# Order of the value products and place of the gate chain in the mixer of a two-layer hybrid block

## Chip, cores and metric

One core of a Trainium2 chip (trn2) runs the whole program. The metric is device time in microseconds (us), 2345.51 us before the change as the median of three runs (2344.53 to 2345.94).

## The reference

Two layers process 256 latent and 256 context tokens of width 1024. Each layer has a gated feed-forward block, a token mixer and a second feed-forward block, with a normalisation behind each. The change concerns the input projection of the mixer and the gates of its mLSTM branch:

```python
(sb, scg, sx, mq, mk, mv, mo, mg, dq, dk, dv, gs, gm, gd) = split_cols(u @ w_in + b_in)
...
g = mg.astype(jnp.float32).reshape(b, t, 4, ML_HEADS).transpose(2, 0, 3, 1)
gates = (g[0], g[1], jax.nn.log_sigmoid(g[2]), jax.nn.log_sigmoid(g[3]))
...
bcum = jnp.cumsum(fc, axis=-1)
d_log = jnp.where(lower, bcum[..., :, None] - bcum[..., None, :] + ic[..., None, :], -jnp.inf)
m_t = jnp.maximum(m_inter, jnp.max(d_log, axis=-1))
```

`mv` are the values (1024 columns, 4 heads), `mg` the 16 gate columns. From the gates come running sums and a running maximum over the tokens, forward and backward; this maximum (the stabiliser) enters the exponentials of the mLSTM scores.

## The kernel before

**Products.** TensorE (PE) multiplies in fp32r, each product in three passes: high part by high part, low by high, high by low. A weight chunk comes by DMA into one of two `raw` buffers. ScalarE (ACT) rounds it into `w_hi` (line 1631) and VectorE (DVE) subtracts to get `w_lo` (line 2365). There are four `w_hi`/`w_lo` slots, so the function `ahead`, called at the step of chunk r, splits chunk r+4 and first waits until chunk r has been multiplied. The DMA of a chunk waits until the chunk two before it has been split.

**The stretch of the change.** `proj_order` writes the order of the steps by hand, and each engine goes through it in order. Behind four `mk` chunks come twelve `mv` steps, and in the list each of these sixteen steps has a number n from 0 to 15, so `mv` step i is n = i+4. The values are made in three groups of four steps, `VALUE_TILES`: here the tokens are the rows of the result, the four token tiles t lie in PSUM banks 0 to 3, and each step adds two of the eight k tiles to all four banks (24 matmuls). The first group is 272 columns wide (256 value columns and the 16 gate columns), the second 512, the third 256.

At a group's last step DVE copies the four banks out to `vaug`, adding the bias (`values`, line 2960). PE starts the next group, or the next chunk in that bank, when the bank is out. Behind the third group come `sx` 1 (bank 0), `sb` 1 (bank 1), four transposes of gate rows (`gates_turn`, line 1434) and `cg` 2, which takes bank 0 again once DVE has evacuated `sx` 1 to `zpad` (line 2913). Then come the mLSTM scores, the second tile of which waits for `em` on ACT (line 1951).

**The gate chain.** `GATES_BEHIND` says behind which n each part of the chain stands. Part 0: PE transposes the gate columns (line 1428), ACT adds the bias, DVE takes absolute values. Part 1: ACT does Exp and Ln (lines 1942 and 1943, each with a table load), then DVE subtracts and copies, with the backward half reversed (lines 2998 to 3002). Part 2: two scans on DVE. Part 3: sums and the transposes' input on DVE (lines 3017 to 3022). Part 4: DVE makes the stabiliser's rounded and reversed copies and the low parts in `neg_g` (lines 3026 to 3030). Parts 0 and 1 stand behind n = 8, the others behind 9, 12 and 15. On every engine a step's `ahead` comes ahead of the gate parts that stand behind it.

In the second layer `sx`, `sb`, `cg`, `mq`, `mo` and `dq` are made for the latent tokens alone (256 columns instead of 512).

Of the kernel before, what the change touches and what calls it, by code (L numbers as in the profile page):

```python
# [18 lines left out]
ACT = mybir.ActivationFunctionType  # L19
ALU = mybir.AluOpType  # L20
# [5 lines left out]
SEG = 256  # L26
# [139 lines left out]
def in_col(tile):  # L166
    return tile * P + (16 if tile >= 36 else 0)
# [6 lines left out]
    return (2, 72 + tile) if tile < 36 else (3, tile - 36)  # L174


GATES_BEHIND = (8, 8, 9, 12, 15)


def proj_order(layer):  # L180

    order = [("mq", i) for i in range(4)] + [("cg", 0), ("sx", 0), ("sb", 0), ("cg", 1)]
    for n in range(16):
        order.append(("mk", n) if n < 4 else ("mv", n - 4))
        if n in (5, 7):
            order.append(("qk_high" if n == 5 else "qk_low", 0))
        order += [("gates", part) for part, behind in enumerate(GATES_BEHIND) if behind == n]

# [35 lines left out]
EVAC_ENGINE = {"mq": "act", "mk": "dve", "mv": "dve", "cg": "act", "sx": "dve", "sb": "dve",  # L224
               "mo": "act", "dv": "dve", "dq": "act", "dk": "act"}
VALUES = {"mv": 0, "dv": 3}
VALUE_TILES = (("mv", 0, 2), ("mv", 4, 4), ("mv", 2, 2), ("dv", 0, 4))
GATE_COLS = 16
VALUE_WIDTH = [n * P + (GATE_COLS if group == 0 else 0) for group, (_, _, n) in enumerate(VALUE_TILES)]
X_ONLY = {"cg", "sx", "sb", "mq", "mo", "dq"}  # L230
# [181 lines left out]
def build(nc, x, c, ctx, c_ctx, w_ada, b_ada, ln_g, ln_b, ffn1_up, ffn1_down, ffn2_up, ffn2_down,  # L412
# [4 lines left out]
    def at(name, shape, dtype, offset=None):  # L417

        size = int(np.prod(shape[1:])) * 4
        if offset is None:  # L420
            offset = spot[0]
            spot[0] += (size + 31) // 32 * 32
        return nc.alloc_sbuf_tensor_at(name, shape, dtype, offset=offset)
# [82 lines left out]
    neg_g = at("neg_g", [P, TOK], F32R, region + 32 * KB + KB // 2)  # L506
# [14 lines left out]
    gt = [at(f"gt{i}", [P, TOK], F32, region + (64 + 2 * i) * KB) for i in range(8)]  # L521
# [106 lines left out]
    def sem(name):  # L628
        return nc.alloc_semaphore(name)
# [29 lines left out]
    bias_landed, v_summed, rot_done, rope_done = (sem(n) for n in ("bias_landed", "v_summed", "rot_done", "rope_done"))  # L659
    mg_done, gate_act, gate_dve, gate_turn = (  # L660
        sem(n) for n in ("mg_done", "gate_act", "gate_dve", "gate_turn"))
    ng_split = sem("ng_split")
    qk_high, qk_ready = sem("qk_high"), sem("qk_ready")
    pv_high, pv_split = sem("pv_high"), sem("pv_split")
    q_high, q_ready, k_high, k_ready = (sem(n) for n in ("q_high", "q_ready", "k_high", "k_ready"))
# [20 lines left out]
    def wait(eng, s, value):  # L686

        if isinstance(value, int) and value <= 0:
            return
        eng.wait_ge(s, value)  # L690
# [5 lines left out]
    def t0_of(layer, x_only=True):  # L696
        return SEG if layer == DEPTH - 1 and x_only else 0
# [132 lines left out]
    def _(sp):  # L830
# [139 lines left out]
        def mixer(layer):  # L970
            base = BASES[layer, "proj"][0]
            src = w_in[layer].rearrange("(k p) n -> p k n", p=P)
            for step in ORDERS[layer]:
                if step[0] in VALUES:
                    slot, _, split_before = raw_place(base + PLANS[layer][step][0], 0)
                    group, k = VALUES[step[0]] + step[1] // 4, step[1] % 4 * 2
                    kind, tile, n = VALUE_TILES[group]
                    col, dst = in_col(SEC[kind] + tile), raw[:, slot, :].rearrange("p (k n) -> p k n", k=2)
# [52 lines left out]
    def _(pe):  # L1031
# [405 lines left out]
        def ml_scores(layer, head, s):  # L1437
            t0 = t0_of(layer)
            u = HEADS * layer + head
            if s == 0:  # L1440
                pe.wait_ge(evac_dve, BASES[layer, "proj"][2] + PLANS[layer]["mv", 11][3] + 1)
                pe.wait_ge(ng_split, layer + 1)
                wait(pe, ht_ready, u)
                for n in range(2):
                    m = pe.matmul(ps[4 + n][:, t0:TOK], head_rows[:, n, head:head + 1].to_broadcast([P, P]),
                                  neg_g[:, t0:TOK], start=True, stop=True)
                m.then_inc(ng_ready, 1)

                pe.wait_ge(qk_ready, u + 1)
                wait(pe, hsum_ready, nth_out(layer, head, 0))  # L1450
            if s == 1:
                pe.wait_ge(gate_act, 5 * layer + 5)
            ts = max(t0, SEG if s >= 2 else 0)
            out, keys = ps[SCORE_ML[s]][:, ts:TOK], slice(s * P, (s + 1) * P)
            q_hi, k_hi = ml_rounded(head)
            pe.matmul(out, k_hi[:, keys], q_hi[:, ts:TOK], start=True, stop=False)
            pe.matmul(out, k_hi[:, keys], qt_low[:, head, ts:TOK], start=False, stop=False)
            pe.matmul(out, kt_low[:, head, keys], q_hi[:, ts:TOK], start=False, stop=True).then_inc(s_ready, 1)
# [154 lines left out]
    def _(act):  # L1613
# [319 lines left out]
        def gates(layer, part):  # L1933
            if part == 0:
                act.wait_ge(mg_done, layer + 1)
                act.wait_ge(gate_in, 16 * 4 * DEPTH)
                act.activation(gt[1][:, :], ps[6][:, :], ACT.Identity, bias=gate_bias[:, layer:layer + 1]
                               ).then_inc(gate_act, 1)
            elif part == 1:

                act.wait_ge(gate_abs, layer + 1)
                link(act.activation(gt[3][64:128, :], gt[3][64:128, :], ACT.Exp, scale=-1.0))
                act.activation(gt[3][64:128, :], gt[3][64:128, :], ACT.Ln, bias=1.0).then_inc(gate_act, 1)

        def ml_gates(layer):

# [395 lines left out]
    def _(dve):  # L2342
        chain = [0]

        def link(ins):

            chain[0] += 1
            ins.then_inc(dve_chain, 1)
            dve.wait_ge(dve_chain, chain[0])
# [586 lines left out]
        def values(layer, step):  # L2936
# [7 lines left out]
            group = VALUES[kind] + i // 4  # L2944
            _, tile, tiles = VALUE_TILES[group]
            first = 2 * BLOCK * (kind == "dv") + tile * P
# [30 lines left out]
        def flip(dst, src):  # L2977

            dve.tensor_copy(dst[:, 0:SEG], rev(src, 0))
            return dve.tensor_copy(dst[:, SEG:TOK], rev(src, 1))  # L2980

        def rev(src, s):
            return src[:, s * SEG:(s + 1) * SEG][:, ::-1]

        def gates(layer, part):
            raw_g, lf, ln1, ia, la = gt[1], gt[2], gt[3], gt[4], gt[5]
            ones, fsum, gmax, top = gt[6], gt[7], gt[2], gt[0]
            if part == 0:

                dve.memset(vaug[:, :, :, 256:257], 1.0)  # L2990
                dve.memset(vaug[:, :, :, 257:258], 0.0)
                dve.wait_ge(gate_act, 5 * layer + 1)
                link(dve.tensor_scalar(ln1[64:128, :], raw_g[64:128, :], -1.0, None, ALU.mult))
                dve.tensor_tensor(ln1[64:128, :], raw_g[64:128, :], ln1[64:128, :], ALU.max).then_inc(gate_abs, 1)
                link(dve.tensor_scalar(lf[64:128, :], raw_g[64:128, :], 0.0, None, ALU.min))
            elif part == 1:
                dve.wait_ge(gate_act, 5 * layer + 2)
                link(dve.tensor_tensor(lf[64:128, :], lf[64:128, :], ln1[64:128, :], ALU.subtract))

                dve.tensor_copy(ia[0:32, :], raw_g[0:32, :])  # L3000
                flip(ia[32:64, :], raw_g[32:64, :])
                dve.tensor_copy(la[0:32, :], lf[64:96, :])
                link(flip(la[32:64, :], lf[96:128, :]))
            elif part == 2:
                if layer == 0:
                    for n in range(2):
                        m = dve.tensor_reduce(fsum[:, n * HEADS:(n + 1) * HEADS],
                                              ident[:, 64 * n:64 * n + 64].rearrange("p (g n) -> p n g", g=2)
                                              [:, 0:HEADS, :], AXX, ALU.add)
                    link(m)  # L3010
                    link(dve.tensor_copy(head_rows[:, :, :], fsum[:, 0:2 * HEADS].rearrange("p (n h) -> p n h", n=2)))
                link(dve.memset(ones[0:64, :], 1.0))
                link(dve.tensor_tensor_scan(fsum[0:64, :], ones[0:64, :], la[0:64, :], 0.0, ALU.mult, ALU.add))
                link(dve.tensor_tensor(ia[0:64, :], ia[0:64, :], fsum[0:64, :], ALU.subtract))
                link(dve.tensor_tensor_scan(gmax[0:64, :], ones[0:64, :], ia[0:64, :], -3.0e38, ALU.mult, ALU.max))
            elif part == 3:
                link(dve.tensor_tensor(fsum[0:64, :], fsum[0:64, :], gmax[0:64, :], ALU.add))
                link(dve.tensor_scalar(gmax[0:64, :], gmax[0:64, :], -1.0, None, ALU.mult))

                dve.tensor_copy(top[0:32, :], ia[0:32, :])  # L3020
                flip(top[32:64, :], ia[32:64, :])
                dve.tensor_copy(top[64:96, :], fsum[0:32, :])
                flip(top[96:128, :], fsum[32:64, :]).then_inc(gate_dve, 1)
            else:
                turned = ones[64:96, :]
                dve.tensor_copy(neg_g[0:32, :], gmax[0:32, :])
                link(flip(turned, gmax[32:64, :]))
                link(dve.tensor_copy(neg_g[64:96, :], turned))
                dve.tensor_tensor(neg_g[32:64, :], gmax[0:32, :], neg_g[0:32, :].bitcast(F32), ALU.subtract)
                dve.tensor_tensor(neg_g[96:128, :], turned, neg_g[64:96, :].bitcast(F32), ALU.subtract  # L3030
                                  ).then_inc(ng_split, 1)

        def ml_scores(layer, head, s):

# [395 lines left out]
```

## Time and profile before

| | |
|---|---|
| median of three runs | 2345.51 us |
| the profiled execution's own time | 2344.44 us |
| its span in the trace | 2342.7 us |
| PE busy | 2316.9 us, 99% of the span |
| DVE busy | 1659.5 us, 71% |
| ACT busy | 1036.4 us, 44% |
| granted TensorE clock | 0.999 of full speed (2.4 GHz) over the span |

In a row of the timeline the first number is the start in us from the span's start, the second the duration in us. Matmuls are pipelined, and their durations overlap: how long one takes in a stream is read from start to start. A bracket at a row's end gives the idle time of the engine just before it and what ended it.

### The profile page before, as it was taken

What the parts mean: (1) busy time and instruction counts of PE and PEld (TensorE: products, weight loads), DVE (VectorE), ACT (ScalarE), POOL (GpSimd) and SP (SyncE); (2) the same over time, 40 slices, a digit from 0 to 9 for tenths busy, and PEclk for the clock granted to TensorE, in tenths of its full rate; (3) what the DMA queues carried; (4) which work ended last, traced back from release to release, by engine and by line L of the source; (5) the groups of instructions that cost most, each with busy time, mean ns of one, the idle gap of its engine ahead of it and who ended that gap; (6) DMA issues with size and microseconds to landing.
All of it is one profiled execution on the core that took longest, in us unless ns stands there. A gap on an engine that the chain in (4) does not pass through costs nothing.

```text
span 2342.7 us, 36077 instructions
## 1 busy us (share of the span) xinstructions
PE 2316.9 (99%) x13078; PEld 2026.9 (87%) x13078; DVE 1659.5 (71%) x2798; ACT 1036.4 (44%) x1773; POOL 194.7 (8%) x184
## 2 busy tenths in 40 slices
PE   8999999999999999999999999999999999999998
PEld 5888889888888888898888898888898898999997
DVE  6999577467767655669885368887665767878876
ACT  5423224435466544363232264322245456756554
POOL 2111000000000000021110000111100000002220
PEclk9999999999999999999999999999999999999999
DMA  8888465232222322338783328775644433656654
GB/s 272 244 248 250 126 213 150 74 108 73 72 68 81 95 83 71 108 93 260 237 245 108 99 74 252 236 235 177 181 117 119 118 100 105 171 142 195 194 160 141
DMA packets 542331, 356.91 MB, mean 152 GB/s; under 512 B 15430, under 2 KB 495216, under 8 KB 542192
## 3 DMA queue, kind: packets, MB, share of 16 engines
q1 hardware_dynamic: 540744, 354.70, 51.8%
q8 instruction: 85, 1.39, 0.2%
q10 hardware_dynamic: 1448, 0.38, 0.1%
q14 instruction: 54, 0.44, 0.1%
HBM read 337.20 MB, written 17.83 MB: 152 GB/s over the span
## 4 chain that ended last, share of the span: by engine, by line
PE 92%; DVE 3%; issue 1%; ACT 1%; DMA 1%; SPq 1%; POOL 0%; DVEq 0%; ACTq 0%; POOLq 0%
PE ps L1118 25%; PE ps L1120 25%; PE ps L1119 25%; PE ps L1417 2%; PE ps L1418 2%; PE ps L1419 2%; PE ps L1131 1%; PE ps L1488 1%; PE ps L1210 1%; PE ps L1211 1%; PE ps L1212 1%; PE ps L1525 1%; DMA raw<-in_w_in 1%; DVE w_lo L2365 1%; PE ps L1133 1%
## 5 line engine op out<-in xcount | busy, mean ns | idle before, releaser
L1631 ACT ACTIVATE w_hi<-raw 128x1024 fp32r<-128x1024 f32 (+3 forms) x438 | 425.1, 971 | 843.4 <-PE ps L1120 619.8
L2365 DVE TENSOR_TENSOR w_lo<-raw,w_hi 128x1024 fp32r<-128x1024 f32 (+3 forms) x438 | 495.2, 1131 | 421.1 <-ACT w_hi L1631 415.6
L1118 PE MATMUL ps<-u_hi,w_hi 128*128 128x512 f32 (+2 forms) x2176 | 777.4, 357 | 4.1 <-DVE zpad L2913 1.7
L1120 PE MATMUL ps<-u_hi,w_lo 128*128 128x512 f32 (+2 forms) x2176 | 772.6, 355 | 0.0
L1119 PE MATMUL ps<-u_lo,w_hi 128*128 128x512 f32 (+2 forms) x2176 | 772.3, 355 | 0.0
L1118 PEld LDWEIGHTS ps<-u_hi,w_hi 128*128 128x128 f32 x2176 | 410.8, 189 | 64.0 <-DVE zpad L2913 2.0
L1120 PEld LDWEIGHTS ps<-u_hi,w_lo 128*128 128x128 f32 x2176 | 410.8, 189 | 58.0
L1119 PEld LDWEIGHTS ps<-u_lo,w_hi 128*128 128x128 f32 x2176 | 411.0, 189 | 55.8
L2774 DVE SCALAR_TENSOR_TENSOR ada_acc<-ada_in_up,cs,ada_acc 128x512 f32<-128x512 f32 x378 | 285.8, 817 | 0.3 <-DMA ada_in_up<-in_w_ada 0.3
L1118 PE MATMUL ps<-g,w_hi 128*128 128x512 f32 (+1 forms) x572 | 206.7, 361 | 0.0
L1120 PE MATMUL ps<-g,w_lo 128*128 128x512 f32 (+1 forms) x572 | 203.8, 356 | 0.0
L1119 PE MATMUL ps<-g,w_hi 128*128 128x512 f32 (+1 forms) x572 | 203.8, 356 | 0.0
L2298 POOL TENSOR_TENSOR fold<-fold 128x512 f32<-128x512 f32 x64 | 89.1, 1393 | 878.0 <-DMA fold<-fold_out 875.5
L1815 ACT ACTIVATE g<-scr 128x512 f32 (+1 forms) x66 | 41.8, 633 | 204.4 <-DVE scr L2684 194.6
L1118 PEld LDWEIGHTS ps<-g,w_hi 128*128 128x128 f32 x572 | 108.0, 189 | 16.8 <-DVE w_lo L2365 0.5
L1119 PEld LDWEIGHTS ps<-g,w_hi 128*128 128x128 f32 x572 | 108.0, 189 | 16.3 <-issue 0.7
L1120 PEld LDWEIGHTS ps<-g,w_lo 128*128 128x128 f32 x572 | 108.0, 189 | 15.5
L1417 PE MATMUL ps<-w_hi,u_hi 128*128 128x512 f32 (+2 forms) x256 | 86.9, 339 | 0.0
L1419 PE MATMUL ps<-w_lo,u_hi 128*128 128x512 f32 (+2 forms) x256 | 86.4, 337 | 0.0
L1418 PE MATMUL ps<-w_hi,u_lo 128*128 128x512 f32 (+2 forms) x256 | 86.4, 337 | 0.0
L2365 DVE TENSOR_TENSOR w_lo<-h,w_hi 128x1024 fp32r<-128x1024 f32 (+2 forms) x66 | 71.5, 1086 | 20.1 <-ACT w_hi L1631 19.7
L2276 POOL TENSOR_TENSOR scr<-h 128x256 f32<-128x256 f32 x3 | 4.0, 1336 | 972.6 <-DVE h L2573 972.6
(388 smaller groups left out, 3672.1 us busy)
## 6 DMA issues: line engine op xcount, KB each, us to landing
raw<-in_ffn_up SPq DMA_DIRECT2D x150, 512.0 KB, 4.7
raw<-in_w_in SPq DMA_DIRECT2D x124, 512.0 KB, 3.8
ada_in_up<-in_w_ada SPq DMA_DIRECT2D x108, 512.0 KB, 4.7
raw<-in_ffn_down SPq DMA_DIRECT2D x67, 384.0 KB, 3.6
fold_out<-ada_acc SPq DMA_DIRECT2D x32, 512.0 KB, 3.4
fold<-fold_out SPq DMA_DIRECT2D x32, 512.0 KB, 5.5
raw<-in_ffn_down SPq DMA_DIRECT2D x42, 320.0 KB, 3.2
h<-in_ffn_up SPq DMA_DIRECT2D x22, 512.0 KB, 4.0
```

The costliest lines, as they stand in the source:

```text
L1118: pe.matmul(ps[bank][:, cols_of], wh, a_hi, start=a, stop=False)
L1119: pe.matmul(ps[bank][:, cols_of], wh, a_lo, start=False, stop=False)
L1120: m = pe.matmul(ps[bank][:, cols_of], wl, a_hi, start=False, stop=b)
L1131: pe.matmul(ps[bank][:, :].rearrange("p (s t) -> p s t", s=2), wh, g[:, :, k, SEG:TOK], start=(first and n == 0), stop=False)
L1417: pe.matmul(ps[t][:, 0:width], u_hi[:, k, own], wh, start=(k == 0), stop=False)
L1418: pe.matmul(ps[t][:, 0:width], u_lo[:, k, own], wh, start=False, stop=False)
L1419: m = pe.matmul(ps[t][:, 0:width], u_hi[:, k, own], wl, start=False, stop=(k == KD - 1))
L1631: act.activation(hi, whole, ACT.Copy).then_inc(hi_done, 1)
L1815: act.activation(g_hi[:, 2 * i + q // 2, t0:TOK], scr[2 + q // 2][:, t0:TOK], ACT.Copy).then_inc(g_hi_done, 1)
L2298: pool.tensor_tensor(fold[:, 0:n, :], fold[:, 0:n, :], fold[:, n:2 * n, :], ALU.add).then_inc(fold_half, 1)
L2365: dve.tensor_tensor(lo, whole, hi.bitcast(F32), ALU.subtract).then_inc(lo_done, 1)
L2774: dve.scalar_tensor_tensor(ada_acc[:, s, :], w, by, ada_acc[:, s, :], ALU.mult, ALU.add).then_inc(ada_mul, 1)
```

## The change

Three things change. The second and the third group of values change places, so the widths come in the order 272, 256, 512. The parts of the gate chain stand behind n = 8, 9, 13, 14, 14, 15. The old part 4 is cut in two: its rounded and reversed copies are now five ACT instructions (new part 4, behind n = 14), and the two subtractions stay on DVE (part 5, behind n = 15). A semaphore `ng_steps` with three counts per layer takes the place of `ng_split`.

```diff
-GATES_BEHIND = (8, 8, 9, 12, 15)
+GATES_BEHIND = (8, 9, 13, 14, 14, 15)
...
-VALUE_TILES = (("mv", 0, 2), ("mv", 4, 4), ("mv", 2, 2), ("dv", 0, 4))
+VALUE_TILES = (("mv", 0, 2), ("mv", 2, 2), ("mv", 4, 4), ("dv", 0, 4))
...
-                pe.wait_ge(ng_split, layer + 1)
+                pe.wait_ge(ng_steps, 3 * layer + 3)
...
+            elif part == 4:
+                gmax, turned = gt[2], gt[6][64:96, :]
+                act.wait_ge(ng_steps, 3 * layer + 1)
+                act.activation(neg_g[0:32, :], gmax[0:32, :], ACT.Copy)
+                for s in range(2):
+                    own, back = (slice(s * SEG, (s + 1) * SEG) for _ in range(2))
+                    act.activation(turned[:, own], gmax[32:64, back][:, ::-1], ACT.Copy)
+                    m = act.activation(neg_g[64:96, own], gmax[32:64, back][:, ::-1], ACT.Copy)
+                m.then_inc(ng_steps, 1)
...
-                link(dve.tensor_scalar(gmax[0:64, :], gmax[0:64, :], -1.0, None, ALU.mult))
+                dve.tensor_scalar(gmax[0:64, :], gmax[0:64, :], -1.0, None, ALU.mult).then_inc(ng_steps, 1)
...
-            else:
+            elif part == 5:
                 turned = ones[64:96, :]
-                dve.tensor_copy(neg_g[0:32, :], gmax[0:32, :])
-                link(flip(turned, gmax[32:64, :]))
-                link(dve.tensor_copy(neg_g[64:96, :], turned))
+                dve.wait_ge(ng_steps, 3 * layer + 2)
                 dve.tensor_tensor(neg_g[32:64, :], gmax[0:32, :], neg_g[0:32, :].bitcast(F32), ALU.subtract)
                 dve.tensor_tensor(neg_g[96:128, :], turned, neg_g[64:96, :].bitcast(F32), ALU.subtract
-                                  ).then_inc(ng_split, 1)
+                                  ).then_inc(ng_steps, 1)
```

Where the instructions stand is shown at two places. The first is DVE in the first layer, from part 1 of the gate chain on. `w_lo` is a weight split, `gt` the gates' buffers, `vaug` a group's evacuation. Before:

```order
L2995 TENSOR_SCALAR gt_127<-gt_126 64x512
L2998 TENSOR_TENSOR gt_127<-gt_127,gt_128 64x512 [waits gate_act,dve_chain]
L3000 COPY gt_129<-gt_126 32x512 [waits dve_chain]
...
L2980 COPY gt_130<-gt_127 32x256
L2365 TENSOR_TENSOR w_lo<-raw,w_hi 128x2x256 [waits chunk_used,hi_done,dve_chain]
L3007 TENSOR_REDUCE gt_132<-con 128x4 x2
...
L2365 TENSOR_TENSOR w_lo<-raw,w_hi 128x2x256 [waits chunk_used,hi_done,dve_chain]
L2960 TENSOR_TENSOR vaug<-ps,value_bias 128x2x256 [waits v_summed,bias_landed]
```

After:

```order
L3004 TENSOR_SCALAR gt_127<-gt_126 64x512
L2374 TENSOR_TENSOR w_lo<-raw,w_hi 128x1024 [waits chunk_used,hi_done,dve_chain]
L3007 TENSOR_TENSOR gt_127<-gt_127,gt_128 64x512 [waits gate_act]
L3009 COPY gt_129<-gt_126 32x512 [waits dve_chain]
...
L2989 COPY gt_130<-gt_127 32x256
L2374 TENSOR_TENSOR w_lo<-raw,w_hi 128x1024 [waits chunk_used,hi_done,dve_chain]
L2969 TENSOR_TENSOR vaug<-ps,value_bias 128x256 [waits v_summed,bias_landed]
```

Part 1 (the row that waits for `gate_act`) stood in the first step of the second group with part 2 between it and that group's evacuation. Now it stands in the second step, one split ahead of the evacuation, and the group's chunks are half as wide.

The second place is ACT in the first layer, from the split at n = 8 on. Before:

```order
L1631 ACTIVATE w_hi<-raw 128x2x256 [waits raw_in0,chunk_used]
L1937 ACTIVATE gt_126<-ps,gate_bias 128x512 [waits gate_in,mg_done]
L1942 ACT_TABLE_LOAD
L1942 ACTIVATE gt_128<-gt_128 64x512 [waits gate_abs]
L1943 ACT_TABLE_LOAD
L1943 ACTIVATE gt_128<-gt_128 64x512 [waits act_chain]
L1631 ACTIVATE w_hi<-raw 128x2x256 [waits raw_in1,chunk_used]
```

After:

```order
L1631 ACTIVATE w_hi<-raw 128x1024 [waits raw_in0,chunk_used]
L1937 ACTIVATE gt_126<-ps,gate_bias 128x512 [waits gate_in,mg_done]
L1631 ACTIVATE w_hi<-raw 128x1024 [waits raw_in1,chunk_used]
L1942 ACT_TABLE_LOAD
L1942 ACTIVATE gt_128<-gt_128 64x512 [waits gate_abs]
L1943 ACT_TABLE_LOAD
L1943 ACTIVATE gt_128<-gt_128 64x512 [waits act_chain]
L1631 ACTIVATE w_hi<-raw 128x1024 [waits raw_in0,chunk_used]
```

Exp and Ln now stand behind the split of the next step, which waits (`chunk_used`) until PE has finished the group's second chunk.

## Rows read from the trace of the kernel before

**Rows 1.** The page: busy time of TensorE, and its granted clock in 40 slices.

```profile
PE 2316.9 (99%) x13078; PEld 2026.9 (87%) x13078; DVE 1659.5 (71%) x2798; ACT 1036.4 (44%) x1773; POOL 194.7 (8%) x184
...
PEclk9999999999999999999999999999999999999999
```

**Rows 2.** Waits of PE: us in total, times, longest us.

```profile
PE ps L1118 <- DVE zpad L2913: 1.7, 1, 1.7
```

**Rows 3.** Timeline of PE, first layer, value groups and the chunk behind them.

```profile
485.67 0.47 PE L1417 MATMUL ps<-w_hi,u_hi 128*128 128x512 f32 x1
...
491.23 0.60 PE L1428 MATMUL ps<-con,gate_rows 128*128 128x128 f32 x4
491.58 0.48 PE L1417 MATMUL ps<-w_hi,u_hi 128*128 128x512 f32 x1
...
519.43 0.28 PE L1419 MATMUL ps<-w_lo,u_hi 128*128 128x256 f32 x1
520.04 0.50 PE L1118 MATMUL ps<-u_hi,w_hi 128*128 128x512 f32 x1 [0.33 <-DVE vaug L2960]
```

**Rows 4.** Timeline of PE, second layer, from the third group's end on.

```profile
1842.88 0.39 PE L1118 MATMUL ps<-u_hi,w_hi 128*128 128x256 f32 x1 [0.36 <-DVE vaug L2960]
...
1848.74 0.60 PE L1434 MATMUL ps<-con,gt 128*128 128x128 f32 x4
1851.05 0.38 PE L1118 MATMUL ps<-u_hi,w_hi 128*128 128x256 f32 x1 [1.71 <-DVE zpad L2913]
...
1854.49 0.28 PE L1458 MATMUL ps<-ada_round,kt_low 128*128 128x256 f32 x1
1855.30 0.39 PE L1456 MATMUL ps<-ada_round,low_round 128*128 128x256 f32 x1 [0.53 <-ACT em L1951]
```

**Rows 5.** Timeline of ACT, first layer, split and Exp and Ln of the gates.

```profile
491.43 0.63 ACT L1631 ACTIVATE w_hi<-raw 128x512 fp32r<-128x512 f32 x1 [4.24 <-PE ps L1419]
...
492.65 1.28 ACT L1942 ACT_TABLE_LOAD   x1
...
495.99 0.63 ACT L1943 ACTIVATE gt<-gt 64x512 f32<-64x512 f32 x1
...
513.99 1.06 ACT L1631 ACTIVATE w_hi<-raw 128x1024 fp32r<-128x1024 f32 x1 [1.82 <-PE ps L1419]
```

**Rows 6.** Timeline of DVE, first layer, gate chain, splits and evacuation.

```profile
496.72 0.69 DVE L2998 TENSOR_TENSOR gt<-gt,gt 64x512 f32<-64x512 f32 x1 [2.37 <-ACT gt L1943]
...
499.33 0.69 DVE L2365 TENSOR_TENSOR w_lo<-raw,w_hi 128x512 fp32r<-128x512 f32 x1
...
513.34 0.68 DVE L3017 TENSOR_TENSOR gt<-gt,gt 64x512 f32<-64x512 f32 x1
...
516.38 1.23 DVE L2365 TENSOR_TENSOR w_lo<-raw,w_hi 128x1024 fp32r<-128x1024 f32 x1
...
519.56 1.41 DVE L2960 TENSOR_TENSOR vaug<-ps,value_bias 128x256 f32<-128x256 f32 x4
```

**Rows 7.** Timeline of DVE, second layer, evacuation, the stabiliser's low parts, split, zpad.

```profile
1831.05 0.69 DVE L2960 TENSOR_TENSOR vaug<-ps,value_bias 128x512 f32<-128x512 f32 x1 [0.67 <-PE ps L1419]
...
1847.96 0.68 DVE L3029 TENSOR_TENSOR neg_g<-gt,neg_g 32x512 fp32r<-32x512 f32 x1
...
1849.38 1.23 DVE L2365 TENSOR_TENSOR w_lo<-raw,w_hi 128x1024 fp32r<-128x1024 f32 x1
1850.52 0.48 DVE L2913 SCALAR_TENSOR_TENSOR zpad<-ps,cols,scr 128x256 f32<-128x256 f32 x1
```

**Rows 8.** Loads of line 871 in the mixer of the second layer, issue to landing.

```profile
DMA to landing us min/median/max: 3.7/3.8/5.0
```

**Rows 9.** PE at the start; last row: five busy times, clock, DMA share, GB/s.

```profile
9.88 3.65 PE L1049 MATMUL ps<-con,x_in 128*128 128x128 f32 x16 [9.88 <-DMA x_in<-in_x]
13.89 1.91 PE L1049 MATMUL ps<-con,x_in 128*128 128x128 f32 x16
...
10.00:12.00 2.00, 2.00 (x10) 2.00 (x11) 0.14 (x1) 0.92 (x2) 0.00 (x0) 1.00 1.04 371
```

More of the change, by code:

```diff
@@ L661, in build @@
         sem(n) for n in ("mg_done", "gate_act", "gate_dve", "gate_turn"))
-    ng_split = sem("ng_split")
+    ng_steps = sem("ng_steps")
     qk_high, qk_ready = sem("qk_high"), sem("qk_ready")
```

## Prediction

> **What bounds the kernel now.** I read the page first. TensorE (PE) is busy for 99% of the span and the granted clock is full in every slice [rows 1], so a change that removes no matmul can only move PE's stops. The table of PE's waits comes next: the longest wait behind the start is 1.7 us, for `zpad` [rows 2]. The timelines of the value groups show where PE stops there: at the end of the third group for `vaug`, in both layers [rows 3, 4], and in the second layer alone for `zpad` and for `em` [rows 4]. These stops are all that can be won: 0.5 us twice, 2.0 and 0.7, together some 3.7 us or 0.16%. A measurement of this kernel can tell about 0.2% (4.7 us) from no change, so no full success of the change would be seen. What it can lose has no such limit. So the question is whether the new order makes PE wait elsewhere, and that is read from the timelines of ACT and DVE, which go through their lists in order.
>
> **PE's pieces.** A chunk of 256 columns: two of them fill 1842.88 to 1848.74, so 2.88 us each with 0.1 for the slower first matmul [rows 4]; one matmul is 0.12. A chunk of 512 columns: 485.67 to 491.23, less 0.1, so 5.45. The four transposes: 491.23 to 491.58, 0.35 [rows 3]. The number of chunks and matmuls stays, so the product work costs the same in the new order.
>
> **Step 1, the border between the second and third group.** PE may start the third group in bank 0 when DVE has evacuated that bank of the second group. The order of instructions shows that DVE now has part 1 of the gate chain and one split ahead of this evacuation, and that ACT makes Exp and Ln only behind the split that waits for the group's second chunk. First layer, from 485.67 on:
>
> - PE: first chunk to 488.55, transposes to 488.90, second chunk to about 491.8. The third and fourth would end at 497.55, and there the third group is due.
> - ACT: the split starts 0.20 behind the chunk's end (491.23 on PE, 491.43 on ACT [rows 3, 5]), at 492.0, and takes 1.06 [rows 5]. The way from the first table load to the end of Ln took 492.65 to 496.62, 3.97 us [rows 5]. So Ln ends at 497.0.
> - DVE: 0.10 to the subtraction (496.62 to 496.72 [rows 5, 6]), 2.61 for part 1 (496.72 to 499.33 [rows 6]), 1.14 for the split (1849.38 to 1850.52 [rows 7]), so the evacuation starts at 500.88.
> - PE goes on 0.48 behind the start of an evacuation 256 wide (519.56 on DVE, 520.04 on PE [rows 3, 6]), at 501.36.
>
> PE stops for 501.36 - 497.55 = 3.8 us. Before, the same chain lay beside chunks of 5.45 us, with three of them between part 0 and the evacuation, and nothing stopped. The second layer has the same instructions there, so the two stops cost **7.6 us**. Queued behind DVE's wait for Ln are that split and the evacuation; it is the evacuation that PE waits for. On both sides I leave 0.4 us per stop, about what one small instruction more or less in this chain is worth.
>
> **Step 2, the end of the third group.** Call the end of its last chunk E. The chunk before ends at E - 5.45. ACT's split starts 0.20 later and takes 1.06, DVE's split takes 1.14, and part 3, now behind this step, takes 3.04 (513.34 to 516.38 [rows 6]). The evacuation of bank 0 therefore starts at E, and PE goes on 0.75 later (0.48, and 0.27 more for 512 columns: 0.69 [rows 7] against 0.42 in the first of the four [rows 6]). Before, PE stopped for 520.04 - 519.43 - 0.12 = 0.49 [rows 3]. That is 0.25 per layer, **+0.5 us** together.
>
> **Step 3, `zpad` and `em` in the second layer.** PE reaches `cg` 2 at E + 0.75 + 5.86 + 0.35 = E + 6.95. DVE has four evacuations of 0.69 to E + 2.75, a split to 3.9, the two subtractions of part 5 (1847.96 to 1849.38, 1.42 [rows 7]) to 5.3, a split to 6.45, and `zpad` lets PE go on 0.53 behind its start (1850.52 on DVE, 1851.05 on PE [rows 4, 7]), at 6.98. So this stop goes: 1848.74 to 1851.05 less the transposes' 0.35 is **-1.96 us**. In the first layer `sx` and `sb` are twice as wide and nothing waited. What ends this stop is partly the shorter part 5, partly that the group before is long. The wait for `em`, 1854.49 to 1855.30 less 0.12, 0.69 [rows 4], I keep. The split ahead of it waits for a load, which took 3.7 to 5.0 us in this layer [rows 8], so it may shrink to 0 or grow by 1.2.
>
> **The rest.** The copies on ACT: at most 0.63 each, the row of 64 by 512 [rows 5], so five are 3.2 us. They start when part 3 has its maximum, near E - 1.9, and end by E + 1.3; DVE asks for them at E + 3.9, so they lie beside DVE's evacuations. No row shows ACT reading in reverse. Were it free, nothing is won; at twice the price they end at E + 4.5 and `zpad` comes 0.6 later. I take the plain price, since the plain rows are the only ones near. SP's loads: those for the second group become half as big, those for the third are wanted while chunks of 2.88 us run. The one that counts is that of the split ahead of Exp: it can start when the split of the fourth narrow chunk is done, near 487.0, and by the slowest row [rows 8] it lands at 492.0, just when ACT wants it. It costs nothing.
>
> **The clock.** The 16 transposes behind PE's first idle 9.88 us took 3.65, later ones of the same form 1.91 [rows 9]: 1.74 us more, nearly a factor of two, though the granted clock reads 1.00 there, the full 2.4 GHz [rows 9]. Behind the idle 1.71 us at 1851.05 the chunk went on at the usual pace: 2.88 us of it and five small matmuls lie ahead of 1854.49 [rows 4]. The new stops of 3.8 us are nearer to 1.71 than to 9.88, so I take 0, with 1.74 per stop as the upper end.
>
> The Trainium skill (TensorE: Matmul & The Clock Gate, section "Why this matters for your kernels") speaks against long gaps between bursts of matmuls, since an idle PE falls back to half its clock. By it both new stops would be followed by slow matmuls, and the sum would be 9.6 instead of 6.1. No run here shows it for gaps of this length.
>
> **The sum.** 7.6 + 0.5 - 1.96 = **+6.1 us**. The profiled execution took 2344.44 us, so its like would take 2350.5; the median of the runs is 1.1 higher, 2345.51, and I put the sum on that: **2351.6 us**. Its own range: 0.8 either way from step 1, 0.7 down and 1.2 up from `em`, 0.3 up for a rest of `zpad`: 2350.1 to 2353.9.
>
> **Rivals.**
>
> - No stop at the border. DVE would have to reach the evacuation 3.8 us earlier, that is Ln would have to end by 493.2. For it: ACT is idle for 4.24 us ahead of the split there [rows 5], so it has time. Against it: the instruction order, in which the split waits for the second chunk, and the rows that price what follows. Then 0.5 - 1.96 = -1.5 remains, 2344.0 us, not slower. Chance 0.12.
> - The clock falls behind both stops: 2 x 1.74 more, 2355.1 us. For it: the program's start [rows 9]; against it: the idle 1.71 us without a trace of it. The chance is 0.08; the skill's rule above is this case.
> - The change does not do what it says at the end: `zpad` still comes late in the second layer, because DVE waits in part 5 for ACT's copies. It decides from copies that take more than 5.8 us (E - 1.9 to E + 3.9), and in full then the 1.96 stays: 2353.6 us. For it: the reversed reads that no row shows; against it: 3.2 us for five plain ones. Chance 0.06.
>
> **How the numbers follow.** The forecast has 0.74, the rivals 0.12, 0.08 and 0.06. The line for slower by over 0.2% is 2350.2, at the low end of the forecast's own range: 0.61 of its 0.74 lie above, 0.13 below. With 0.08 and 0.06 slower is 0.75. The first rival gives 0.10 to no change and 0.02 to faster, so these are 0.23 and 0.02. The range from 2347.5 to 2355.5 holds nearly all of the forecast and the two slower rivals, 0.85, and leaves out the first rival.
>
> **What would show it.** In the profile of the changed kernel PE's table of waits should have a new head: `vaug`, twice near 3.8 us, at the first matmul of the third group, near 497.5 in the first layer. ACT's Ln should end near 497.0, and on DVE a split should stand between part 1 and the four evacuations 256 wide. The wait for `zpad` should be gone from the second layer, and `vaug` behind the third group should read some 0.6 in each. I am wrong if PE runs through the border of the groups, if the clock or the pace of the matmuls falls behind the stops, or if a load makes ACT late at the split ahead of Exp.

## The result, and the profile after

The changed kernel takes 2355.15 us, the median of six runs (2353.37 to 2357.22), against 2345.27 for the kernel before in the same session: a ratio of 1.0043, interval 1.0033 to 1.0053, or 9.9 us slower. The forecast was 6.1 slower, 2351.6 us, with 2355.1 for the rival in which the clock falls behind both stops. The profiled execution took 2356.55 us, 2354.8 of them in its span. In its page PE is busy longer than before [rows 1] though it does the same work:

```profile
PE 2321.9 (99%) x13078; PEld 2029.7 (86%) x13078; DVE 1657.0 (70%) x2790; ACT 1040.8 (44%) x1783; POOL 193.8 (8%) x184
...
PEclk9999999999999999999999999999999999999999
```

The page's slices of 59 us still show a 9 for the clock; what happened lasts 3 to 6 us and is hidden in them. PE's waits (us in total, times, longest) have the new head that the forecast named, and `zpad` [rows 2] is gone:

```profile
PE ps L1417 <- DVE vaug L2969: 7.1, 2, 3.6
...
PE ps L1118 <- DVE vaug L2969: 1.1, 2, 0.6
...
PE ps L1456 <- ACT em L1960: 0.4, 1, 0.4
```

The timeline of PE at the border of the second and third group, first layer, then the same place in the second:

```profile
498.26 0.28 PE L1419 MATMUL ps<-w_lo,u_hi 128*128 128x256 f32 x1
502.10 0.77 PE L1417 MATMUL ps<-w_hi,u_hi 128*128 128x512 f32 x1 [3.57 <-DVE vaug L2969]
502.67 0.63 PE L1418 MATMUL ps<-w_hi,u_lo 128*128 128x512 f32 x1
503.10 0.63 PE L1419 MATMUL ps<-w_lo,u_hi 128*128 128x512 f32 x1
...
505.23 0.44 PE L1418 MATMUL ps<-w_hi,u_lo 128*128 128x512 f32 x1
505.50 0.40 PE L1419 MATMUL ps<-w_lo,u_hi 128*128 128x512 f32 x1
...
1826.82 0.28 PE L1419 MATMUL ps<-w_lo,u_hi 128*128 128x256 f32 x1
1830.67 0.77 PE L1417 MATMUL ps<-w_hi,u_hi 128*128 128x512 f32 x1 [3.57 <-DVE vaug L2969]
...
1836.35 0.47 PE L1418 MATMUL ps<-w_hi,u_lo 128*128 128x512 f32 x1
1836.66 0.39 PE L1419 MATMUL ps<-w_lo,u_hi 128*128 128x512 f32 x1
```

Two things stand here. The stop is 3.72 us (502.10 - 498.26 - 0.12, the time that one matmul of 256 columns takes in the stream). And behind it the matmuls start 0.43 us apart, and only from 505.50 on 0.23 apart, the pace of the kernel before. The granted clock by stretch says why (us, busy time of PE, PEld, DVE, ACT and POOL, clock, DMA share, GB/s; the first three rows from the first layer, the others from the second):

```profile
502.00:504.00 2.00, 1.90 (x5) 1.54 (x6) 2.00 (x4) 0.00 (x0) 0.00 (x0) 0.50 0.50 130
504.00:506.00 2.00, 2.00 (x8) 1.58 (x7) 0.08 (x1) 0.00 (x0) 0.00 (x0) 0.67 0.77 203
506.00:508.00 2.00, 2.00 (x10) 1.66 (x9) 0.00 (x0) 0.00 (x0) 0.00 (x0) 1.00 0.69 199
...
1830.60:1833.00 2.40, 2.33 (x6) 1.88 (x7) 2.05 (x4) 0.00 (x0) 0.00 (x0) 0.50 0.67 178
1833.00:1836.00 3.00, 3.00 (x9) 2.32 (x8) 0.00 (x0) 0.00 (x0) 0.00 (x0) 0.50 0.76 210
```

Behind the stops PE runs at 0.50, that is 1.2 GHz. Eight matmuls from 502.10 to 505.50 took 3.40 us instead of 8 x 0.23 = 1.84: 1.6 us lost. Fourteen from 1830.67 to 1836.66 took 5.99 instead of 3.22: 2.8 us.

Who made PE wait stands on ACT and DVE as foretold. ACT, then DVE, first layer:

```profile
492.82 1.06 ACT L1631 ACTIVATE w_hi<-raw 128x1024 fp32r<-128x1024 f32 x1 [1.68 <-PE ps L1419]
493.89 1.28 ACT L1942 ACT_TABLE_LOAD   x1
...
497.13 0.63 ACT L1943 ACTIVATE gt<-gt 64x512 f32<-64x512 f32 x1
```

```profile
497.79 0.69 DVE L3007 TENSOR_TENSOR gt<-gt,gt 64x512 f32<-64x512 f32 x1 [2.60 <-ACT gt L1943]
...
500.40 1.23 DVE L2374 TENSOR_TENSOR w_lo<-raw,w_hi 128x1024 fp32r<-128x1024 f32 x1
501.54 1.41 DVE L2969 TENSOR_TENSOR vaug<-ps,value_bias 128x256 f32<-128x256 f32 x4
```

ACT's split waits for PE's second chunk, Exp and Ln with their table loads follow, and DVE, which waits for Ln, has part 1 and a split ahead of the evacuation that PE needs.

### The profile page after: what moved, and what is told of

The parts are those of the page before. It is cut to its first block, busy times and chain, and to the rows that moved or that the text cites. A ratio compares the mean times of both kernels' runs of the same rounds, so it can differ in the third digit from the quotient of the medians.

```text
span 2354.8 us, 36077 instructions
## 1 busy us (share of the span) xinstructions
PE 2321.9 (99%) x13078; PEld 2029.7 (86%) x13078; DVE 1657.0 (70%) x2790; ACT 1040.8 (44%) x1783; POOL 193.8 (8%) x184
## 4 chain that ended last, share of the span: by engine, by line
PE 91%; DVE 3%; ACT 2%; DMA 2%; issue 2%; POOL 0%; DVEq 0%; SPq 0%; ACTq 0%; POOLq 0%
PE ps L1118 25%; PE ps L1120 25%; PE ps L1119 25%; PE ps L1131 1%; PE ps L1417 1%; PE ps L1418 1%; PE ps L1419 1%; PE ps L1488 1%; PE ps L1210 1%; PE ps L1212 1%; PE ps L1211 1%; DVE w_lo L2374 1%; PE ps L1525 1%; PE ps L1133 1%; DMA raw<-in_w_in 1%
```

## The experiments

Each is compared with the kernel before, run in the same session; two versions from different sessions are compared by what each lies above or below its own kernel before. The theory: the change costs two stops at the border, made by Ln and part 1 ahead of the evacuation, and a fall of the clock behind each. The rivals put the loss elsewhere: on the copies, on the order of the groups as such, or on late operands instead of the clock.

**Fill the stop with matmuls.** The changed kernel, with 16 more matmuls ahead of the third group, into a bank where nobody reads them.

```diff
+                if kind == "mv" and i == 8 and t == 0:
+                    for _ in range(16):
+                        pe.matmul(ps[5][:, 0:BLOCK], u_hi[:, 0, own], w_hi[:, slot, 0:BLOCK], start=True, stop=True)
```

> The changed kernel with 16 more matmuls of 512 columns on PE ahead of the third group, into a bank that nothing reads then; their result is not used. They fill the stop of 3.7 us. Theory (the clock falls because PE is idle): the third group still starts when vaug is out, but at the full clock, 0.23 us from matmul to matmul; 2355.2 - 4.2 = 2351.0 us. Rival (the matmuls behind the stop are slow because DVE's evacuation and splits and the loads run beside them): the first seven to fourteen matmuls of the third group stay at 0.43 us, 2355 us.

Measured: 2350.39 us, ratio 1.0023 (1.0014 to 1.0032). DVE's evacuation is where it was and PE still goes on late, but the clock does not fall, in either layer:

```profile
502.00:504.00 2.00, 2.00 (x10) 1.62 (x10) 1.78 (x3) 0.00 (x0) 0.00 (x0) 1.00 0.76 195
...
1830.00:1833.00 3.00, 3.00 (x14) 2.45 (x14) 1.33 (x2) 0.00 (x0) 0.00 (x0) 1.00 0.74 193
```

So the slow matmuls come from PE's idleness, not from late operands or from DVE's work beside them: they cost 9.9 - 5.4 = 4.5 us by the medians, each against its own kernel before, and 4.4 (1.6 and 2.8) read from the timeline. The 5.4 that is left is near what the forecast had summed without a fall of the clock (6.1).

**The copies back on DVE.** The kernel before with the new order and `GATES_BEHIND = (8, 9, 13, 14, 15)`, five parts, the old part 4 with its copies on DVE.

> The changed kernel with the stabiliser's rounded and reversed copies back on DVE, behind n = 15 with the two subtractions; order of the values and the other places as in the change. Theory (the copies on ACT shorten DVE's way to zpad in the second layer by 1.4 us and touch nothing else): the stops and the fall of the clock stay, zpad is waited for again by 1.2 to 1.5 us in the second layer, 2356.5 us. Rival (what removed the wait for zpad is the long third group, not the copies' engine): no wait for zpad, 2355.2 us.

Measured: 2355.1 us, 1.0042 (1.0028 to 1.0055), the same as the changed kernel within the noise; five executions from 2353.13 to 2358.0 can't tell the theory's 2356.5 from the rival's 2355.2. The trace speaks against both in part: the `zpad` wait is back, with 0.8 us instead of 1.2 to 1.5, and the `em` wait is gone from the list. The border stands unchanged:

```profile
PE ps L1417 <- DVE vaug L2960: 7.1, 2, 3.6
...
PE ps L1118 <- DVE zpad L2913: 0.8, 1, 0.8
```

So the loss is not in the copies. Of what ScalarE's copies save ahead of `zpad`, PE loses about half at `em` in this version: from the four transposes to the matmul that needs `em` it takes 4.97 us here (1864.05 to 1869.02) and 4.47 in the changed kernel (1861.86 to 1866.33).

**The copies alone.** The changed kernel with the old order of groups and the old places of the parts:

```diff
-GATES_BEHIND = (8, 9, 13, 14, 14, 15)
+GATES_BEHIND = (8, 8, 9, 12, 14, 15)
...
-VALUE_TILES = (("mv", 0, 2), ("mv", 2, 2), ("mv", 4, 4), ("dv", 0, 4))
+VALUE_TILES = (("mv", 0, 2), ("mv", 4, 4), ("mv", 2, 2), ("dv", 0, 4))
```

> The changed kernel with the old order of the value groups (272, 512, 256 columns) and the old places of the chain's parts: of the change, the copies by ScalarE alone. Theory: VectorE's last part loses its four copies (some 1.4 us), so zpad comes 1.4 us sooner in the second layer and the zpad stop of 2.0 us falls to about .65; nothing else moves, and the clock does not fall: 2345.0 less 1.4, 2343.6. Rival (the copies are late on ScalarE behind its splits, and the subtraction waits for them): the stop stays, 2345.0.

Measured: 2344.18 us, 0.9997 (0.9988 to 1.0006): no difference clear of the noise, and the theory's 1.4 us lie inside the interval. In the profiled execution the theory's stop shrank as expected, from 1.96 to 0.61 (1850.08 - 1849.12 - 0.35), and its gain did not arrive. PE, second layer, and the clock behind the last row:

```profile
1849.12 0.60 PE L1434 MATMUL ps<-con,gt 128*128 128x128 f32 x4
1850.08 0.38 PE L1118 MATMUL ps<-u_hi,w_hi 128*128 128x256 f32 x1 [0.36 <-DVE zpad L2922]
...
1856.13 0.54 PE L1456 MATMUL ps<-ada_round,low_round 128*128 128x256 f32 x1 [2.33 <-ACT em L1960]
...
1856.00:1860.00 4.00, 3.87 (x19) 3.87 (x20) 2.86 (x6) 3.35 (x9) 0.00 (x0) 0.57 0.56 137
```

ACT there, and the same split in the kernel before:

```profile
1852.57 1.06 ACT L1631 ACTIVATE w_hi<-raw 128x1024 fp32r<-128x1024 f32 x1 [4.75 <-DMA raw<-in_w_in]
...
1855.69 0.38 ACT L1960 ACTIVATE em<-ps 128x256 f32<-128x256 f32 x1
```

```profile
1851.73 1.06 ACT L1631 ACTIVATE w_hi<-raw 128x1024 fp32r<-128x1024 f32 x1 [4.26 <-DMA raw<-in_w_in]
```

The wait for `em` grew from 0.53 [rows 4] to 2.33, because ACT makes `em` behind a split that waits for a load. The split starts 3.45 us behind the transposes here (1852.57 - 1849.12) and 2.99 before (1851.73 - 1848.74 [rows 4]). The load is issued 2.1 us ahead of the transposes in both, behind a split of DVE that precedes the shortened part, so the copies can't bring it forward; it took 5.0 us before and 5.5 here. While it is that long, a shorter `zpad` stop only brings PE to it sooner. The clock fell behind this wait too, which cost some 1.6 us more (16 matmuls from 1856.13 on took 3.5 us instead of 1.9), and this execution, 2346.47, is the second slowest of eleven. None of the faster ones was profiled, so whether some of the gain arrives in them stays open.

**The order alone.** The kernel before with the new `VALUE_TILES` line of the change's diff only.

> The kernel before with one line of the change, the new order of the value groups alone; the chain keeps its five parts and their places, and the copies stay on VectorE. Parts 1 and 2 of the chain, with the wait for Exp and Ln, then both stand ahead of the second group's evacuation on VectorE. Theory: the stop ahead of the third group is about 7 us in the first layer and 6.5 in the second, the granted clock falls to 0.50 behind both (1.5 and 2.7 us), the vaug stops at the end of the third group go (-1) and the zpad stop shrinks to some .3 us (-1.8): about 2345 + 13.5 + 4.2 - 2.8 = 2360. Rival (part 2 finds its operands ready and costs the evacuation nothing): the stop stays at 3.7 us, and the time at 2353 to 2355.

Measured: 2358.54 us, 1.0057 (1.0042 to 1.0073). With parts 1 and 2 ahead of the evacuation the stops reach 7.0 and 6.5 us, and PE goes on at half the clock behind both:

```profile
PE ps L1417 <- DVE vaug L2960: 13.6, 2, 7.0
...
504.40:506.40 2.00, 2.00 (x5) 1.61 (x6) 1.94 (x4) 0.00 (x0) 0.00 (x0) 0.50 0.63 167
...
1835.25:1837.25 2.00, 2.00 (x5) 1.61 (x6) 1.98 (x4) 0.00 (x0) 0.00 (x0) 0.50 0.60 149
```

**The places and the copies, without the order.** The changed kernel with the old order:

```diff
-VALUE_TILES = (("mv", 0, 2), ("mv", 2, 2), ("mv", 4, 4), ("dv", 0, 4))
+VALUE_TILES = (("mv", 0, 2), ("mv", 4, 4), ("mv", 2, 2), ("dv", 0, 4))
```

> The changed kernel with the old order of the value groups (272, 512, 256) and the new places of the chain's parts. Part 1 with its wait for Ln then stands ahead of the evacuation of some of the 512-column group, which has 20 us of matmuls behind it, and part 3 ahead of the 256-column group's evacuation. Theory: TensorE stops 5 to 5.6 us at the end of the 256-column group in each layer, because part 3 stands ahead of its evacuation, the granted clock falls to 0.50 behind both stops (1.5 to 2.7 us each), and the zpad stop is gone (-2): about 2345 + 10.6 + 4 - 2 = 2357. Rival (it is the order of the groups that costs, and the new places of the chain cost nothing of themselves): 2343 to 2346.

Measured: 2356.68 us, 1.0052 (1.0037 to 1.0068), as expected. The narrow group is the third again, and the stop stands at its end, where part 3 is ahead of its evacuation, with the clock at 0.50 after it:

```profile
PE ps L1118 <- DVE vaug L2969: 10.4, 2, 5.4
...
525.80:528.00 2.20, 2.16 (x5) 1.77 (x6) 2.17 (x5) 0.86 (x1) 0.00 (x0) 0.50 0.00 0
```

So the order, and the rest of the change, each cost no less alone than together: 13.6 and 11.9 us by the medians against 9.9, with intervals that overlap. In these three versions what decides is how much of the chain stands inside the narrow group, ahead of its evacuation.

**The split behind the evacuation.** The changed kernel, DVE's split of `mv` step 6 one place later:

```diff
+            if kind == "mv" and i == 6:
+                return
...
+            if kind == "mv" and i == 7:
+                ahead(base, r - 1, width=value_width(r - 1 + SPLIT))
```

> The changed kernel with one VectorE step moved: the split of mv step 6 (1.2 us of w_lo, 128x1024), which in the changed kernel stands ahead of the second group's evacuation, goes behind it. The evacuation then ends about 1.2 us sooner in each layer, and the stop of TensorE ahead of the third group falls from 3.7 to about 2.55 us. That is 2 x 1.2 = 2.4 us off 2355.15. Theory (the fall of the granted clock to 0.50 behind each stop, worth 1.5 and 2.7 us, needs a stop somewhere between 1.7 and 3.6 us; a stop of 2.55 lies between, and either side is open): 2352.7 if the clock still falls behind it, 2348.5 if it does not. Rival (the slow matmuls behind the stop come from VectorE's and TensorE's shared use of memory or from late operands, not from the clock): the .43 us spacing of the third group stays whatever the granted clock says, 2352.7.

Measured: 2348.82 us, 1.0014 (1.0005 to 1.0023), eleven executions from 2346.72 to 2351.26. The stop is 2.43 us of idle time, as foreseen. The median is near the 2348.5 of a clock that holds, but in the profiled execution, the slowest of the eleven, it fell:

```profile
500.75:502.00 1.25, 1.25 (x3) 1.06 (x4) 1.25 (x4) 0.00 (x0) 0.00 (x0) 0.50 0.07 13
...
1827.80:1830.00 2.20, 2.18 (x6) 1.77 (x7) 2.20 (x5) 0.00 (x0) 0.00 (x0) 0.63 0.03 7
```

So a second profile was taken of the same version.

> The version with the split of mv step 6 behind the second group's evacuation, unchanged, profiled once more. Its eleven executions spread from 2346.7 to 2351.3, twice as far as those of the versions without a stop, and the profiled one, in which the clock fell behind both stops of 2.43 us, was the slowest of them. Theory (a stop of 2.43 us lets the clock fall in some executions and not in others): a profiled execution near 2347 to 2349 shows the granted clock at 1.00 behind one stop or both, and .23 us spacing there; one near 2351 shows 0.50 behind both again. Rival (the clock falls behind both stops always, and the spread has another cause): 0.50 behind both stops, whatever the time.

Measured: 2350.73 us, 1.0021 (1.0011 to 1.003), from 2346.95 to 2352.16. This profiled execution took 2351.07 and the clock fell behind both stops again, as theory and rival both allow:

```profile
502.00:504.00 2.00, 2.00 (x6) 1.52 (x6) 1.85 (x2) 0.00 (x0) 0.00 (x0) 0.50 0.11 18
...
1829.00:1831.00 2.00, 2.00 (x6) 1.59 (x5) 1.91 (x2) 0.00 (x0) 0.00 (x0) 0.52 0.11 18
```

What speaks here is the mean clock of each of the 21 executions of this version: 0.999 in the seven that took 2346.7 to 2348.2, 0.998 in nine from 2348.6 to 2351.1, 0.997 in five from 2350.9 to 2352.2. The filled version, without an idle stop, has 0.999 in all its eleven; the kernel before has 0.999 or 0.998 in the experiments' sessions, never 0.997. So a stop of 2.43 us seems to take the clock down in some executions and not, or for less time, in others. That is argued from the means, of which 0.998 alone tells nothing; an execution in which the clock held was not profiled.

**Part 1's copies behind the evacuation.** The changed kernel, with part 1's subtraction where it was and its six copies on DVE behind the evacuation.

```diff
-
+            elif part == "copies":
...
+                    if step == ("mv", 7):
+                        gates(layer, "copies")
```

> The changed kernel with part 1 of the gates' chain cut in two: its sum of 64x512 stays ahead of the second group's evacuation, its six copies on VectorE go behind it. The evacuation then ends about 2 us sooner, and the stop of TensorE ahead of the third group falls from 3.7 to about 1.75 us in each layer. Theory (the granted clock falls behind a stop of 3.6 us and, as behind the zpad stop of 1.7 us in the kernel before, not behind one this short): the stops give back 2 x 1.95 = 3.9 us and the slow matmuls 4.2 us, 2347.0. Rival (the clock falls behind any stop at that place): 2351.2. A second rival (the later copies make the later parts of the chain late, as when the whole chain was moved back): the stop at the end of the third group grows past .73 us and takes back 1 to 2 us.

Measured: 2349.09 us, 1.002 (1.001 to 1.0029). Both theory and rival had the stop wrong: it is 2.10 us idle, not 1.75, since DVE's split now waits 0.45 us for ACT's, which stands behind Ln. In the profiled execution (2351.59) the clock fell behind both stops of 2.10 us too:

```profile
498.97 1.23 DVE L2374 TENSOR_TENSOR w_lo<-raw,w_hi 128x1024 fp32r<-128x1024 f32 x1 [0.45 <-ACT w_hi L1631]
...
500.68 0.76 PE L1417 MATMUL ps<-w_hi,u_hi 128*128 128x512 f32 x1 [2.10 <-DVE vaug L2969]
...
500.68:502.00 1.32, 1.32 (x3) 1.13 (x4) 1.32 (x4) 0.00 (x0) 0.00 (x0) 0.50 0.39 81
...
1829.35:1831.90 2.55, 2.55 (x7) 1.96 (x7) 1.69 (x6) 0.00 (x0) 0.00 (x0) 0.51 0.83 222
```

The median lies between the theory's 2347.0 and the first rival's 2351.2, as with the split. The second rival is out: PE's two waits for `vaug` behind the third group stay at 0.6 us.

**The chain later.** The changed kernel with `GATES_BEHIND = (8, 12, 13, 14, 14, 15)`: part 1 behind the first step of the third group.

> The changed kernel with one number moved: part 1 of the gate chain behind n = 12 instead of 9, so that DVE has no wait for Ln ahead of the second group's evacuation. Theory (part 1's place makes the stop of 3.7 us in each layer, and the idle time makes the clock fall behind it, 1.5 and 2.7 us): both go, 2355.2 - 7.4 - 4.2 = 2343.5 us, no wait of PE for vaug at the third group's start, granted clock 1.00 there. Rival (the narrow second group itself leaves DVE too little time for its splits and the evacuation, wherever the chain stands): a wait for vaug of over 1 us stays in each layer, 2348 us or more.

Measured: 2345.73 us, 1.0002 (0.9993 to 1.0011). The border is clear and the clock holds, but the theory missed by 2.2 us: parts 1 to 3 now stand close together behind n = 12 to 14, and part 3 makes the third group's evacuation late:

```profile
PE ps L1118 <- DVE vaug L2969: 2.7, 2, 1.6
...
521.60:524.00 2.40, 2.38 (x10) 1.98 (x11) 2.40 (x4) 0.57 (x1) 0.00 (x0) 1.00 0.00 0
```

It shows as well that the clock held behind an idle 1.60 us.

**The chain spread.** `GATES_BEHIND = (8, 11, 12, 13, 13, 14)`: part 1 behind the second group's last step, past the evacuation, and parts 3 and 4 one step ahead of the third group's.

> The changed kernel with the parts behind n = 8, 11, 12, 13, 13, 14: part 1 behind the second group's evacuation, part 3 ahead of the third group's last chunk. Theory: no stop at the border and no fall of the clock as in the run with part 1 behind n = 12, and DVE is free when the third group's banks fill, so the two waits for vaug at its end (0.7 us each) go as well: 2343.5 - 1.4 = 2342.1 us, 3 us under the kernel before. Rival (the chain is now so early that DVE is late with the splits for the third group): PE waits for w_lo there, no better than 2345.

Measured: 2342.33 us, 0.9988 (0.9979 to 0.9997), as expected. What is left is a `vaug` wait of 0.46 us in the first layer, where the last part stands ahead of the evacuation.

**The last part behind n = 15.** The same with `(8, 11, 12, 13, 13, 15)`. (The time 318.25 in the text is 518.25.)

> The changed kernel with the parts of the chain behind steps 8, 11, 12, 13, 13 and 15: as the version that spread them behind 8, 11, 12, 13, 13, 14 and took 2342.3, but for the last part (the subtraction, 318.25 to 519.6 in the first layer's row of times, ahead of the third group's last evacuation there), which goes behind step 15. Theory: the vaug stop left in the first layer (.62 us, .46 of it a wait for vaug) goes, and zpad is still ready in time in the second layer: 2341.7. Rival: the zpad stop comes back in the second layer by as much as the subtraction is later, .5 to 1.1 us: 2342.3 to 2343.

Measured: 2340.93 us, 0.9982 (0.9973 to 0.9991): 4.0 us below the kernel before, the fastest of all. PE passes both borders without a `vaug` wait, and the clock stays at 1.00 behind the border:

```profile
497.70:500.00 2.30, 2.30 (x11) 1.90 (x11) 1.60 (x4) 1.76 (x2) 0.00 (x0) 1.00 0.67 169
...
1849.69 1.06 ACT L1631 ACTIVATE w_hi<-raw 128x1024 fp32r<-128x1024 f32 x1 [2.33 <-DMA raw<-in_w_in]
...
1853.25 0.39 PE L1456 MATMUL ps<-ada_round,low_round 128*128 128x256 f32 x1 [0.22 <-ACT em L1960]
```

The last two rows tell why the gain at `zpad` counts here and did not in the profile of the copies alone: with the wide group last, the load is issued earlier and the split ahead of `em` starts 0.72 us behind the transposes (at 1848.97) instead of 2.99, so `em` costs PE 0.22 us. The 4.0 us won are about what the prediction had summed as all that can be won, 3.7. It held that too little to be told from no change; with eleven executions the interval leaves 1 out.

**The same places, copies on DVE.** The kernel before with the new order and `GATES_BEHIND = (8, 11, 12, 13, 15)`.

> The kernel before with the new order of the value groups and its five parts behind steps 8, 11, 12, 13 and 15: the version that took 2340.9, but with the four copies on VectorE, at step 15. Theory: no stop at either border of the groups, no fall of the clock; the last part on VectorE is some 1.4 us longer, so zpad comes that much later in the second layer, where it had about .3 us to spare: a zpad stop of about 1.1 us comes back, 2342.0. Rival (the copies fit in VectorE's idle time, so that moving them to ScalarE brings nothing): 2340.9.

Measured: 2341.87 us, 0.9986 (0.9977 to 0.9995). PE waits for `zpad` again, 0.6 us instead of the 1.1 expected:

```profile
PE ps L1118 <- DVE zpad L2913: 0.6, 1, 0.6
```

So order and places bring some 2.9 us (2344.77 - 2341.87). The copies on ScalarE bring a further 1.1 by the medians (4.0 against 2.9), but the two intervals overlap: that last step is seen in the trace, not in the times.

## Why the prediction was right, and what it missed

- **The border (step 1), right.** Forecast: Ln ends at 497.0, PE is due at 497.55 and stops for 3.8 us. Measured: 497.76, 498.38 and 3.72. The shift of 0.8 is the first load, which ended PE's first idle time at 10.7 instead of 9.88 [rows 9]. With 3.73 in the second layer that is 7.45 for 7.6.
- **The third group's end (step 2), right.** PE waits 0.57 and 0.56 for `vaug`, 0.33 and 0.36 before [rows 3, 4]: +0.4 for +0.5.
- **`zpad` and `em` (step 3), right in size.** The `zpad` wait is gone, `em` keeps 0.42 of 0.53 [rows 4]. The rival with late copies is out. ACT reads in reverse at about the plain price: 256 columns in 0.40 to 0.42 us, where `em`, 256 columns in plain order, took 0.38.

```profile
523.68 0.63 ACT L1947 ACTIVATE neg_g<-gt 32x512 fp32r<-32x512 f32 x1 [2.40 <-DVE gt L3027]
524.32 0.42 ACT L1950 ACTIVATE gt<-gt 32x256 f32<-32x256 f32 x1
524.64 0.40 ACT L1951 ACTIVATE neg_g<-gt 32x256 fp32r<-32x256 f32 x1
```

- **The clock, the step that failed.** The prediction took 0 with 1.74 per stop as the upper end, because 3.8 us is nearer to the idle 1.71 without a fall than to 9.88. The runs show a fall behind an idle 3.57, and behind 2.10, 2.33 and 2.43 too, worth 1.6 and 2.8 us in the profiled execution, and none when the stop is filled. A nearer row on one side is no evidence on which side of a step a value lies; the rival with a chance of 0.08 came true. Its price, from the start's transposes, was near for one stop and low for the other. The 1.00 that the prediction read beside these transposes [rows 9] was no measurement: the trace's record of the clock begins only at 13.7 us, where their pace doubles, and a stretch without a record reads 1.00. Their pace ahead of it, 3.65 us against 1.91 for sixteen, fits a clock at 0.50, and so the row spoke for the rival more plainly than it was taken to.

The rule quoted with it (the Trainium skill, TensorE: Matmul & The Clock Gate, "Why this matters for your kernels"), that an idle PE falls back to half its clock, agrees with the trace: 0.50 behind 3.57 us. By it the sum was 9.6, and 9.9 was measured.

That the numbers meet so well is partly luck. The measured 2355.15 lies outside the forecast's own range (2350.1 to 2353.9) and inside the wide one only because that was drawn to hold the rivals; and the rival's 2355.1 has 3.5 us for the clock, where the profiled execution shows 4.4.

The profiled execution gives 7.45 + 4.4 + 0.4 - 1.96 - 0.1 = 10.2, and 0.8 for the first load. Its span is 12.1 longer than the one before; the other 1.1 us are small differences spread over the span, which I don't assign. The medians differ by 9.9.

## What to carry to other kernels

On an engine that goes through a list, an instruction that waits for a long chain elsewhere belongs behind whatever the bottleneck needs next: here another set of six places, with part 1 past the evacuation, turned 9.9 us lost into 4.0 won. Price a new stop of TensorE at its length and, in a kernel like this one, some 1.5 to 3 us more for the clock behind it, unless a row shows that one of that length passes. Before counting the gain of a stop removed, look for the next thing that PE will meet: at `em` it was a load, and in the profiled execution the whole gain went there.

## What the runs showed of the hardware

- Granted clock behind a stop of PE in a busy stream: 1.00 in profiled executions behind an idle 1.60 and 1.71 us, and 0.50 behind 2.10, 2.33, 2.43, 3.57, 5.39 and 7.01 us. At 2.43 the means of 21 executions differ, 0.997 to 0.999.
- What the fall costs did not follow the stop's length: 1.6 and 2.8 us behind two stops of 3.57 us, and about 2.0 behind 7.01 us.
- The slow pace can begin after some matmuls at full pace: behind the second stop of the split version three matmuls ran at full pace, so that the clock of the first 2.2 us is 0.63 in the mean.
- ScalarE's copy of 32x256 with the columns reversed took 0.40 us, and Ln began 0.01 us behind its table load of 1.28 us.
